# First dilated attention of a two-layer decoder: casts of keys and queries seven units ahead, softmax shares on GpSimd and ScalarE, turned rows at the head of each step

## The reference

```
D_MODEL = 1024; SEQ = 1024; DEC_BATCH = 8; HEAD_DIM = 64; A_HEADS = 8
A_GROUPS = ((128, 1), (512, 4), (2048, 16))       # window, dilation

def a_mixer(hn, pos, caches, w_in, q_g, k_g, w_out):
    qkv = (hn @ w_in).reshape(n, T, 3, N_GROUPS, A_HEADS, HEAD_DIM)
    for g, (window, dil) in enumerate(A_GROUPS):
        q = rope(rms_norm(qkv[:, :, 0, g], q_g[g]), pos)
        k = rope(rms_norm(qkv[:, :, 1, g], k_g[g]), pos)
        v = qkv[:, :, 2, g]
        if caches is None:
            o, lse = dilated_attention_prompt(q, k, v, window, dil)
        else:
            o, lse, new = dilated_attention_sample(q, k, v, caches[g], window, dil)
    wts = jax.nn.softmax(jnp.stack(lses, axis=0), axis=0)     # shares of the three groups
    o = jnp.einsum('gnthd,gnth->nthd', jnp.stack(outs, axis=0), wts)
    return o.reshape(n, T, A_HEADS * HEAD_DIM) @ w_out, rows   # rows: new caches
```

## Time and profile before

| what | value |
|---|---|
| time before | 2952.8 us, the median of 2965.94, 2952.64 and 2952.8 |
| profiled execution | 2953.42 us; span of its trace 2951.6 us |
| granted TensorE clock, mean | 0.949 |
| PE busy | 2710.9 us (92%) |
| DVE busy | 1736.7 us (59%) |
| ACT busy | 985.1 us (33%) |
| POOL busy | 725.0 us (25%) |

### The profile page before, as it was taken

The page is one execution under the profiler, slowest core; times in us unless marked ns, Lnnn a source line. Parts: engine busy times, 40 slices in busy tenths (PEclk is TensorE's granted clock), DMA queues, the critical chain, the costliest instruction groups (busy, mean ns, idle before and its releaser), DMA issues.

```text
span 2951.6 us, 45737 instructions
## 1 busy us (share of the span) xinstructions
PE 2710.9 (92%) x17524; PEld 2636.7 (89%) x17524; DVE 1736.7 (59%) x2732; ACT 985.1 (33%) x1826; POOL 725.0 (25%) x342
## 2 busy tenths in 40 slices
PE   4999999788687999999999969698979999999997
PEld 3999999677676999999999958588979999999997
DVE  6887831555455555555555586695255655555655
ACT  3666631765303212221222245484222121112120
POOL 2111121333303222222222132173232222222220
PEclk7999999898788999999999989898999999999998
DMA  3322233443244343433354211344623444434441
GB/s 104 88 75 86 72 108 101 140 140 110 83 129 113 84 96 82 89 82 89 82 105 94 49 39 46 122 162 126 127 51 83 98 95 91 97 84 82 96 75 61
DMA packets 219856, 275.64 MB, mean 93 GB/s; under 512 B 29562, under 2 KB 191746, under 8 KB 217666
## 3 DMA queue, kind: packets, MB, share of 16 engines
q1 hardware_dynamic: 219746, 274.17, 37.2%
HBM read 237.90 MB, written 125.62 MB: 123 GB/s over the span
## 4 chain that ended last, share of the span: by engine, by line
PE 81%; DVE 8%; ACT 3%; DMA 3%; issue 2%; POOL 1%; SPq 1%; DVEq 0%; ACTq 0%; POOLq 0%
PE acc L347 23%; PE acc L349 23%; PE acc L348 23%; DVE arena L579 2%; PE aux L1869 2%; PE aux L1502 2%; PE acc L1461 1%; PE acc L1856 1%; PE acc L1470 1%; DVE arena L555 1%; PE acc L1839 1%; PE aux L635 1%; PE aux L634 1%; PE acc L2100 1%; POOL xl L533 1%
## 5 line engine op out<-in xcount | busy, mean ns | idle before, releaser
L347 PE MATMUL acc<-xh,w_hi 128*128 128x344 f32 x3504 | 1136.8, 324 | 63.4 <-DVE xl L533 36.3
L349 PE MATMUL acc<-xh,w_lo 128*128 128x344 f32 x3504 | 1127.8, 322 | 0.0
L348 PE MATMUL acc<-xl,w_hi 128*128 128x344 f32 x3504 | 1127.4, 322 | 0.0
L332 POOL TENSOR_TENSOR w_lo<-w_raw,w_hi 128x1024 fp32r<-128x1024 f32 x194 | 485.5, 2507 | 1799.9 <-ACT w_hi L322 1799.9
L347 PEld LDWEIGHTS acc<-xh,w_hi 128*128 128x128 f32 x3504 | 665.8, 190 | 82.0 <-issue 39.6
L349 PEld LDWEIGHTS acc<-xh,w_lo 128*128 128x128 f32 x3504 | 665.8, 190 | 0.0
L348 PEld LDWEIGHTS acc<-xl,w_hi 128*128 128x128 f32 x3504 | 665.8, 190 | 0.0
L849 DVE TENSOR_TENSOR hT<-hT,acc 128x1032 f32<-128x1032 f32 x184 | 226.3, 1230 | 387.6 <-PE acc L349 387.6
L322 ACT CAST w_hi<-w_raw 128x1024 fp32r<-128x1024 f32 x194 | 201.8, 1050 | 603.2 <-PE acc L349 504.3
L347 PE MATMUL acc<-f_hi,w_hi 128*128 128x344 f32 x1056 | 340.2, 322 | 11.1 <-DVE f_lo L1108 11.1
L349 PE MATMUL acc<-f_hi,w_lo 128*128 128x344 f32 x1056 | 339.5, 321 | 0.0
(11 more groups left out here) (254 smaller groups left out, 3184.6 us busy)
## 6 DMA issues: line engine op xcount, KB each, us to landing
out_a_w_sample<-in_cache_a_kv_w SPq DMA_DIRECT2D x23, 2848.0 KB
w_raw<-in_ffn_w_up SPq DMA_DIRECT2D x88, 512.0 KB, 3.8
scratch<-arena SPq DMA_DIRECT2D x46, 516.0 KB, 3.1
w_raw<-in_ffn_w_down SPq DMA_DIRECT2D x44, 512.0 KB, 3.5
w_raw<-in_a_w_in SPq DMA_DIRECT2D x36, 512.0 KB, 4.3
out_a_w_sample<-in_cache_a_kv_w SPq DMA_DIRECT2D x8, 2044.0 KB
arena<-in_cache_a_kv_w SPq DMA_DIRECT2D x24, 512.0 KB, 3.8
w_raw<-scratch SPq DMA_DIRECT2D x18, 512.0 KB, 3.7
```

The source lines that it names most:

```text
L332: pool.tensor_tensor(w_lo[:, slot, :], w_raw[:, slot, :], w_hi[:, slot, :].bitcast(F32), ALU.subtract).then_inc(lo_ready, 1)
L347: pe.matmul(out, whi, ahi, start=first, stop=False)
L348: pe.matmul(out, whi, alo, start=False, stop=False)
L349: return pe.matmul(out, wlo, ahi, start=False, stop=last)
```

## The change

The change has five parts, all in the first attention and its edges.

1. The first group's keys, queries and values are read back at chunk 26 of the projection and cast at chunk 29 (`FIRST_SPLIT`), into tiles that are free there. The scores of the first two units wait for the projection's last parts alone.
2. The casts of the later groups stand at the end of a step, seven units before the group's first one (eight for the third group), where they stood three and two before it and ahead of the exponentials. Their loads, the value and key rows' places and the tables move along.
3. The turned key rows are copied out on VectorE, between the two halves of a unit's mask.
4. Of the shares the two minima stay on VectorE. The difference, the sums and the product go to GpSimd, and the reciprocal becomes a logarithm and an exponential on ScalarE. The weights follow one step later.
5. TensorE's turned rows stand at the head of a step, ahead of the scores. The decode tokens' columns, queries, cache rows and first two spreads are moved into the last pair's steps.

```
-        K_JOBS = ((2, 0, 7, 1), (3, 1, 4, 4), (6, 2, 0, 4), (7, 2, 4, 4))
+        K_JOBS = ((-7, 0, 7, 1), (-2, 1, 4, 4), (2, 2, 0, 4), (4, 2, 4, 4))
+        def split_at(x):
+            return first_a(x) - (7, 7, 8)[x % NG]
...
-                names += [("w", i, r - 5, half) for half in range(2)] if 5 <= r < 8 else []
+                names += [("w", i, r - 6, half) for half in range(2)] if 6 <= r < 9 else []
+            if 38 <= k < 38 + NG:
+                names += [("sq", k - 38)]
...
-        ON_ACT = {"v": False, "k": True, "stat": True, "w": False}
+        ON_ACT = {"v": False, "k": False, "stat": True, "w": False, "sq": False}
...
             else:
-                pe.wait_ge(acc_evac, 3 * CH_B)
+                pe.wait_ge(acc_evac, 3 * CH_B - (2 if u else 3))
...
+        def shares_pool(pool, i):
+            if i:
+                wait_job(pool, ("w", i - 1, 2, 1))
+            n, s = a_st[:, :, 0, :], 7 * i
+            pool.wait_ge(DA.w_step, s + 2)
+            pool.tensor_tensor(a_e, n, a_min.unsqueeze(1).to_broadcast([16, NG, P]), ALU.subtract) \
                 .then_inc(DA.w_step, 1)
...
+        def sums_pool(pool, i):
+            d, s = a_st[:, :, 1, :], 7 * i + 3
+            pool.wait_ge(DA.w_exp, 3 * i + 1)
+            pool.tensor_tensor(d, d, a_e, ALU.mult).then_inc(DA.w_step, 1)
+            pool.wait_ge(DA.w_step, s + 1)
+            pool.tensor_tensor(a_min, d[:, 0], d[:, 1], ALU.add).then_inc(DA.w_step, 1)
+            pool.wait_ge(DA.w_step, s + 2)
+            pool.tensor_tensor(a_min, a_min, d[:, 2], ALU.add).then_inc(DA.w_step, 1)
+        def sums_act(act, i):
+            act.wait_ge(DA.w_step, 7 * i + 6)
+            act.activation(a_min, a_min, ACT.Ln).then_inc(DA.w_exp, 1)
+            act.wait_ge(DA.w_exp, 3 * i + 2)
+            act.activation(a_min, a_min, ACT.Exp, scale=-1.0).then_inc(DA.w_exp, 1)
+        def weights_pool(pool, i):
+            pool.wait_ge(DA.w_exp, 3 * i + 3)
+            pool.tensor_tensor(a_e, a_e, a_min.unsqueeze(1).to_broadcast([16, NG, P]), ALU.mult).then_inc(DA.w_step, 1)
...
         def attn_a_act(act):
-                for x in starting(k + 3):
-                    if x:
-                        split_a_act(act, x, "k")
-                for x in starting(k + 2):
-                    if x:
-                        split_a_act(act, x, "q")
                 if 0 <= k < A_UNITS:
                     exps_a_act(act, k, 0)
-                i, r = divmod(k, 10)
-                if 0 <= i < A_PAIRS and r in (2, 3, 6, 7):
-                    key_rows_act(act, 4 * i + (2, 3, 6, 7).index(r))
                 i, r = divmod(k - 10, 10)
                 if 0 <= i < A_PAIRS and r == 1:
                     stats_act(act, i)
+                if 0 <= i < A_PAIRS and r == 4:
+                    sums_act(act, i)
...
                 if 0 <= i < A_PAIRS and r == 3:
                     shares_act(act, i)
+                for x in splitting(k):
+                    split_a_act(act, x, "k")
+                for x in splitting(k - 1):
+                    split_a_act(act, x, "q")
...
         def attn_a_pool(pool):
+                if 0 <= i < A_PAIRS and r == 3:
+                    shares_pool(pool, i)
+                if 0 <= i < A_PAIRS and r == 4:
+                    sums_pool(pool, i)
+                if 0 <= i < A_PAIRS and r == 5:
+                    weights_pool(pool, i)
+                for x in splitting(k):
                     split_a_lo(pool, x, "k")
...
-            attn_a_pe(pe)
+            attn_a_pe(pe, -1, A_TAIL)
+            sample_first_pe(pe)
+            attn_a_pe(pe, A_TAIL, A_STEPS)
             sample_a_pe(pe)
```

More of the change, by code:

```diff
@@ L759, in proj_a_sp @@
                     store_chunk(sp, CH + e + BODY * i, e % 2, scratch[e + BODY * i])
-            for n in range(A_CHUNKS - BODY, A_CHUNKS):
+            for n in range(24, A_CHUNKS):
+                if n == 26:
+                    first_loads_sp(sp)
+                    first_values_sp(sp)
                 if n + 3 < A_CHUNKS:
@@ L1229, in group_a, with splitting, key_jobs_at @@
             return NG * i + g, r - A_FIRST[g]
+        def split_at(x):
+            return first_a(x) - (7, 7, 8)[x % NG]
+        def splitting(k):
+            return [x for x in range(1, A_GRP) if split_at(x) == k]
+        def key_jobs_at(k):
+            return [4 * i + n for i in range(A_PAIRS) for n in range(4)
+                    if k == (10 * i + K_JOBS[n][0] if 10 * i + K_JOBS[n][0] > 0 else (2, 0)[n])]
         def starting(k):
@@ L1266, in jobs_at @@
                 names += [("v", x, 0), ("v", x, 1)]
-            i, r = divmod(k, 10)
-            if 0 <= i < A_PAIRS:
-                names += [("k", 4 * i + n) for n in range(4) if K_JOBS[n][0] == r]
+            names += [("k", n) for n in key_jobs_at(k)]
             i, r = divmod(k - 10, 10)
@@ L1285, in build @@
                 order_a.append(name)
+        key_order = [name[1] for name in order_a if name[0] == "k"]
         def bank_a(name):
@@ L1330, in raw_a, with landed_a, key_job_of, first_loads_sp @@
         def raw_a(x, what):
-            return k_raw[x % 2] if what == "k" else q_raw
+            if x == 0:
+                return a_og["kqv".index(what)]
+            if what == "k":
+                return w_raw[:, 0, :] if x % 2 else w_lo[:, 2, :].bitcast(F32)
+            return w_raw[:, 2, :] if what == "q" else w_hi[:, 2, :].bitcast(F32)
+        def landed_a(eng, x, what):
+            if what == "k":
+                eng.wait_ge(DA.k_in[(x + 1) % 2 if x else 2], 16 * ((x + 1) // 2) if x else 16)
+            elif what == "q":
+                eng.wait_ge(DA.q_in[x > 0], 16 * max(x, 1))
+            else:
+                eng.wait_ge(DA.v_in[x > 0], 16 * max(x, 1))
         def rows_in_scratch(w, x):
             return scratch[12 * w + 4 * (x % NG) + x // NG, :, 0:SEQ]
+        def key_job_of(x):
+            return [n for n in range(4 * A_PAIRS) if NG * (n // 4) + K_JOBS[n % 4][1] == x][-1]
+        def first_loads_sp(sp):
+            sp.wait_ge(chunk_out, 3 * (CH + 24))
+            sp.wait_ge(stored[0], 16 * 12)
+            sp.wait_ge(stored[1], 16 * 12)
+            sp.dma_start(raw_a(0, "k"), rows_in_scratch(1, 0)).then_inc(DA.k_in[2], 16)
+            sp.dma_start(raw_a(0, "q"), rows_in_scratch(0, 0)).then_inc(DA.q_in[0], 16)
+        def first_values_sp(sp):
+            sp.wait_ge(stored[0], 16 * 13)
+            sp.dma_start(raw_a(0, "v"), rows_in_scratch(2, 0)).then_inc(DA.v_in[0], 16)
         def attn_a_loads(sp, x, what):
             if what == "q":
-                if x:
+                if x > 1:
                     sp.wait_ge(DA.kq_lo, 2 * x)
@@ L1578, in probs_a @@
             wait_job(eng, ("t", u, e))
+            if u == 0:
+                for n in range(2):
+                    eng.wait_ge(stored[n], 16 * A_CHUNKS // 2)
             if u >= 2:
@@ L1624, in weigh_dve, with key_rows_dve, attn_a_dve @@
                                  bank_a(("w", i, g, half)), ALU.mult).then_inc(DA.out_dve, 1)
-        def attn_a_dve(v_):
-            for k in range(A_STEPS):
+        def key_rows_dve(v_, n):
+            cnt = K_JOBS[n % 4][3]
+            wait_job(v_, ("k", n))
+            turn, stage = divmod(key_order.index(n), 2)
+            if turn:
+                v_.wait_ge(DA.k_out[stage], 16 * turn)
+            else:
+                v_.wait_ge(lo_ready, U_AOUT + 2)
+            v_.tensor_copy(k_stage[stage][:, 0:P * cnt], bank_a(("k", n))[:, 0:P * cnt]).then_inc(DA.out_dve, 1)
+        def attn_a_dve(v_, k0, k1):
+            for k in range(k0, k1):
                 for x in range(A_GRP):
@@ L1632, in attn_a_dve @@
                 if k < A_UNITS:
-                    mask_a_dve(v_, k)
+                    mask_a_dve(v_, k, 0)
                 if k == 0:
-                    for n in range(2):
-                        v_.wait_ge(stored[n], 16 * A_CHUNKS // 2)
                     v_.memset(a_vt[:, :, :, HD:2 * HD].rearrange("p b t c -> p (b t) c"), 0.0).then_inc(DA.cleared, 1)
@@ L1639, in attn_a_dve @@
                     value_rows_dve(v_, x)
+                for n in key_jobs_at(k):
+                    key_rows_dve(v_, n)
                 i, r = divmod(k - 10, 10)
-                if 0 <= i < A_PAIRS and 5 <= r < 8:
-                    weigh_dve(v_, i, r - 5)
+                if 0 <= i < A_PAIRS and 6 <= r < 9:
+                    weigh_dve(v_, i, r - 6)
+                if 38 <= k < 38 + NG:
+                    sample_rows_dve(v_, k - 38)
+                if k < A_UNITS:
+                    mask_a_dve(v_, k, 1)
                 if 0 <= k - 2 < A_UNITS:
```

312 lines of the change are left out of this document (154 added, 158 removed).

## The result

The changed kernel takes 2940.6 us (median of 13 runs, 2938.89 to 2944.87); the kernel before, run beside it, 2954.2 (13 runs). The ratio is 0.9944, with an interval from 0.9928 to 0.9959: 0.6% faster, some 14 us, where 46 were forecast.

A forecast was written before the change was run, and what follows sets the result against it. TensorE, busy 92% of the span, bounds the kernel; its waits and half-clock time around the first attention can be gained. Start 14, pairs 20.5 and tail 12 sum to 46.5 us: from 2953.4 to 2907, range 2885 to 2932.

The forecast's parts named there:

- The start (A): Stretch before the first attention's first statistics: they come at 568 instead of 582.4, gaining 14 us (8 to 18).
- the base of the sum: At the start: VectorE's last copies return to normal, so ScalarE is free for the attention from about 520.9.
- I count 2.5 us of waiting: At the start: ScalarE's waiting for the second group's keys, added to its 43.2 us of work.
- The pairs (B): The first attention's three head pairs: 58.5, 58.5 and 50 us between statistics, gaining 20.5 us (0 to 37).
- the 18.4 us of waits away: In the pairs: moving casts and key copies removes TensorE's nine waits for ScalarE's key-row copy, 18.4 us.
- What is late next is the chain of the shares: In pairs with casts: minima to product takes 15.65 us through GpSimd and ScalarE, stalling TensorE 7 us.
- at the weights 9 us after the minima: In the pairs: TensorE reaches the weights some 9 us after the minima, then waits 7 us.
- The tail (C): From the last statistics to the output projection's first piece: gains 12 us (5 to 17).
- The step that makes VectorE's products the price of the late minima: At the tail: VectorE's two products, sums and last copy precede the last minima, which begin about 781.5 instead of 778.47.
- The edits at nothing: Columns' load has twelve steps of cover; cache rows' loads cost the last statistics 1 us at most.
- Other waits take the place of those removed: Rival, in the pairs: ScalarE at the logarithm holds up copies, pairs stay near 62 us, time 2927; chance 0.14.
- The start does not move: Rival, at the start: the second group's keys hold the rest, gain there 4 us, time 2917; chance 0.08.

The follow-up runs named there:

- e6: e3 with the load of queries on SyncE one step later still; 2913.5 us.
- e7: Changed kernel with only the key rows' jobs moved apart, every second step in each pair; 2934.9 us.
- e1: Changed kernel with the statistics' transfers ahead of the step's loads of keys and queries on SyncE; 2925.2 us.
- e3: Changed kernel with everything of a step (statistics, stores, value loads) ahead of its loads of keys and queries on SyncE; 2943.6 us.
- e4: Changed kernel with GpSimd's two remainders inside the shares' chain moved one step later, behind the sums and the product; 2930.5 us.
- e10: Changed kernel with the decode tokens' first two spreads, products and head sums behind the last weights again; 2947.8 us.
- e8: Changed kernel with the edits of e6, e4 and e7 together; 2904.0 us.
- e9: e8 with the shares and reciprocal back on VectorE and GpSimd's remainders placed as in the changed kernel; 2916.0 us.
- e2: Changed kernel with key rows' stores and values' loads ahead of the step's loads on SyncE, the statistics still behind; 2956.5 us.
- e11: e8 with the decode tokens' first two steps behind the last weights again; 2926.1 us.

## Why the prediction was wrong

**The start (A), 14 us: measured 2.6.** VectorE's last copy is at its normal 0.34 us again and ScalarE's casts begin at 519.70, so the base of the sum was right. ScalarE's work was near the count too, 46.10 us from 519.3 to 579.7. The step "I count 2.5 us of waiting" failed: 60.40 − 46.10 = 14.3 us of that stretch are ScalarE's waits. The step left out that SyncE stands for GpSimd (e6: 9.2 us) and that the key rows' five jobs, which the new table bunches into steps 0 to 4, go through two staging tiles (e7: 4.1 us alone, 0.4 us beside e6). With both mended the start gives 12.2, inside the range of 8 to 18, with 50.90 − 43.50 = 7.4 us of waiting left.

**The pairs (B), 20.5 us: measured −0.3.** The third pair was forecast at 50 and took 51.2. The two with casts were forecast at 58.5 and took 68.8 and 67.8. What failed is the step that takes "the 18.4 us of waits away" and says "What is late next is the chain of the shares". The waits for key-row copies are 20.3 us, since VectorE itself stands for the statistics and the stores ahead of them: first came the statistics that feed the chain. The prediction looked at SyncE's queue for the decode tokens' loads only; what the moved loads of keys and queries wait for there, and what stands behind them, it did not count. Taking that away is worth 6.3 and 7.3 us for the statistics (e1), up to 9.6 in all (e3).

The chain itself was counted well. In the first pair its product and the weights are:

```profile
614.19 0.99 POOL L1713 TENSOR_TENSOR arena<-arena 16x384 f32<-16x384 f32 x1
...
615.67 2.05 PE L1525 MATMUL acc<-arena,sel 16*128 16x128 f32 x16
```

The minima end at 600.22 and the product at 615.18, 15.0 us later, where 15.65 were counted. In the last pair it is 784.53 − 778.36 = 6.17 from the minima to the weights where 6.0 was counted, with GpSimd's operations at 0.98 and 0.44 us where 0.95 and 0.32 were. But TensorE was not at the weights 9 us after the minima: it came at 615.67 − 600.22 = 15.45 and found them ready. Its stall stands at another place, ahead of a copy of probabilities that ScalarE holds back at the logarithm. Taking the remainders out of the chain alone is worth 4.6 and 6.3 us (e4) against 7. Two readings under B are off as well, without changing its sum: of the 18.4 us 6.1 lie in the start and not in the pairs, and the third pair took 57.9 before and not 62.5, so that 50 would have been 8 us less there and not 12.5.

**The tail (C), 12 us: measured 13.2.** The size is right, and so are its steps, but for one: VectorE's two products and sums lie ahead of the minima, which begin 10.8 us after the statistics (11.6 forecast); the weights to the mix's end take 797.18 + 2.50 − 784.53 = 15.15 (15.1 forecast), and the first piece follows at once. The mix's last remainder:

```profile
797.18 2.50 POOL L1856 TENSOR_TENSOR xl<-arena,xh 128x512 fp32r<-128x512 f32 x2
```

The step that makes VectorE's products the price of the late minima was luck in part: without them the minima still begin 10.1 us after the statistics (e10), because these come back late.

**The edits at nothing.** The early casts lie beside the projection: TensorE is busy 319.30 of 319.30 us from 200 to 519.3 us, in the changed kernel as in the one before.

**The rivals.** Two came true at once. "Other waits take the place of those removed": the sum of the pairs did not change, though its mechanism, ScalarE at the logarithm, is only the smaller part. "The start does not move": A is 2.6 where it had 4, though not for the second group's keys alone. Together they give 2953.4 − 4 − 12 = 2937, near the 2938.9 of the profiled execution; the prediction weighed each by itself.

The forecast is nearest to e6, in which only the queue is mended and the remainders stay in the chain: first statistics at 570.6 (568 forecast), pairs of 60.5, 57.5 and 52.7 us (58.5, 58.5 and 50), 2913.5 us (2907). That e8's 2904 is still nearer to 2907 is luck: its remainders are out of the chain, which the forecast had in it.

## What to carry to other kernels

When a consumer is moved ahead, its loads move on the queue that issues them, and the question for each is what it waits for there and what stands behind it: here one tile of queries made SyncE wait for GpSimd, and small transfers on which all engines depended went out 11 us late. Put loads that must wait for a tile behind everything else of the step, or a step later, and look at the issuing engine's own timeline for gaps. A table that bunches jobs must be counted against the tiles through which they leave (4.1 us here, as long as the stores stood in the queue).

## What the runs showed of the hardware

A VectorE operation of 0.55 us became one of 3.08 us beside GpSimd's remainder (e9, above). The prediction had weighed such a clash for the projection's last copies alone. In the first pair of the kernel before, where no remainder lies beside the shares, the same operations took 0.54 and 0.55 us.

TensorE can run at half clock for a long time while it is busy without a gap. In e3 the output projection from 840 us on was at 1.2 GHz in three windows in a row (columns as in the earlier trace rows):

```profile
840.00:860.00 20.00, 20.00 (x83) 20.00 (x83) 1.42 (x3) 0.00 (x0) 0.00 (x0) 0.50 0.24 79
860.00:880.00 20.00, 20.00 (x84) 20.00 (x83) 1.54 (x3) 0.00 (x0) 0.00 (x0) 0.50 0.24 70
880.00:900.00 20.00, 20.00 (x91) 20.00 (x90) 1.02 (x2) 0.00 (x0) 0.00 (x0) 0.50 0.37 120
```

In e4 the same stretch, behind a stage of nearly the same form, starts at 2.4 GHz, with 151 matmuls in the first 20 us where e3 has 83:

```profile
840.00:860.00 20.00, 20.00 (x151) 20.00 (x151) 2.57 (x5) 0.00 (x0) 0.00 (x0) 1.00 0.45 135
```

The 60 us of e3 held 258 matmuls, which at the pace of e4's window take about 34 us (an estimate from these rows), so some 26 us were lost there. From the first piece to the end the trace of e3 has 2955.0 − 790.02 = 2165.0 us and that of e2, in which the clock is 0.50 from 840 to 900 us too, 2165.4, where the changed kernel has 2137.4; e11 has 2149.9. The executions of e3 lie between 2923.9 and 2956.8 us, those of e2 between 2935.2 and 2964.8, and the traced one is the slowest of each. That the same loss spreads the executions that were not traced is likely, but not shown. In e3 the third pair too took 58.2 us, with no longer waits than in the changed kernel, at a clock of 0.81 where that has 0.93. What decides which level such a stretch starts at was not found: the busy time ahead of it (12.2 of 20 us in both) was the same. The prediction did not depend on it, since from the first piece to the end the kernel before took 2951.6 − 815.25 = 2136.4 us and the changed one 2937.1 − 799.73 = 2137.4.
